# First table's rows eight ahead of the second table's, searches and a gelu moved with them

## The reference

```
def peer_ffn(xn, wq, keys1, keys2, U, V):
    ...
        q = (xc @ wq).reshape(B, C, PEER_HEADS, PEER_DQ)
        ...
        sc, ci = lax.top_k(cand, K)
        e = jnp.take_along_axis(i1, ci // K, axis=-1) * PEER_NKEYS + jnp.take_along_axis(i2, ci % K, axis=-1)
        g = jax.nn.softmax(sc, axis=-1).astype(xc.dtype)
        a = jax.nn.gelu(jnp.einsum('bchkd,bcd->bchk', U[e], xc), approximate=False)
        return jnp.einsum('bchk,bchkd->bcd', g * a, V[e])
```

## Time and profile before

| what | value |
|---|---|
| median of 3 runs | 2156.09 us (2155.67 to 2157.33) |
| the profiled execution's own time | 2158.93 us |
| its span, first to last instruction | 2157.2 us |
| busy PE / DVE / POOL / ACT | 86% / 60% / 34% / 27% of the span |
| gather queue q0 | 537.35 MB in 74176 packets, 60.1% of the 16 DMA engines' span |
| all DMA | 699.82 MB, mean 324 GB/s |
| granted TensorE clock, mean | 0.996 of full speed |

### The profile page before, as it was taken

The page is one execution under the profiler, slowest core; times in us unless marked ns, Lnnn a source line. Parts: engine busy times, 40 slices in busy tenths (PEclk is TensorE's granted clock), DMA queues, the critical chain, the costliest instruction groups (busy, mean ns, idle before and its releaser), DMA issues.

```text
span 2157.2 us, 22090 instructions
## 1 busy us (share of the span) xinstructions
PE 1864.7 (86%) x6535; PEld 1096.5 (51%) x6535; DVE 1286.2 (60%) x2142; ACT 588.8 (27%) x1064; POOL 728.2 (34%) x636
## 2 busy tenths in 40 slices
PE   9999999999999999999977777777777777777777
PEld 7888887777788786544423222222222222222222
DVE  5544556787866556776356556556556556546444
ACT  5544445555544443111111111111111111111101
POOL 2000011110000002755455445445455545545542
PEclk9999999999999999999999999999999999999999
DMA  7556743434456578999999999999999999999997
GB/s 266 190 186 198 225 150 108 146 108 136 139 180 236 188 237 309 398 412 403 421 422 420 422 421 422 422 422 422 422 422 422 422 422 422 422 422 421 422 422 329
DMA packets 164609, 699.82 MB, mean 324 GB/s; under 512 B 15633, under 2 KB 25905, under 8 KB 98257
## 3 DMA queue, kind: packets, MB, share of 16 engines
q0 software_dynamic: 74176, 537.35, 60.1%
q1 hardware_dynamic: 90384, 161.89, 23.4%
q10 hardware_dynamic: 2, 0.01, 0.0%
HBM read 697.10 MB, written 2.10 MB: 324 GB/s over the span
## 4 chain that ended last, share of the span: by engine, by line
PE 50%; DMA 38%; issue 5%; DVE 5%; POOL 1%; ACT 0%; DVEq 0%; POOLq 0%; ACTq 0%
DMA v_ring<-in_peer_v_dram,idx_v 31%; PE banks L1253 10%; PE banks L788 9%; PE banks L790 9%; PE banks L789 9%; DMA big<-in_peer_u_dram,idx_u 7%; PE banks L1222 4%; PE banks L764 1%; PE banks L1143 1%; DVE big L2358 1%; POOL v_ring L643 1%; DVE mx L1990 1%; DVE ws L1832 1%; DVE att L1987 1%; PE banks L1190 1%
## 5 line engine op out<-in xcount | busy, mean ns | idle before, releaser
L1253 PE MATMUL banks<-v_ring,kxT 128*128 128x512 f32 x1920 | 885.4, 605 | 266.7 <-DMA v_ring<-in_peer_v_dram,idx_v 265.7
L2358 DVE SCALAR_TENSOR_TENSOR big<-big,xn 128x2048 f32<-128x2048 f32 x256 | 586.9, 2293 | 417.4 <-DMA big<-in_peer_u_dram,idx_u 409.0
L1253 PEld LDWEIGHTS banks<-v_ring,kxT 128*128 128x128 f32 x1920 | 348.3, 190 | 801.3 <-ACT kxT L1736 390.2
L634 POOL DMA_INDIRECT big<-in_peer_u_dram,idx_u x256 | 369.9, 1445 | 203.8 <-DVE big L2358 109.2
L1832 DVE TENSOR_TENSOR ws<-wraw,ws 128x1024 fp32r<-128x1024 f32 (+1 forms) x248 | 294.6, 1194 | 210.2 <-ACT ws L1373 208.2
L643 POOL DMA_INDIRECT v_ring<-in_peer_v_dram,idx_v x240 | 283.0, 1179 | 404.5 <-PE banks L1253 360.4
L1736 ACT ACTIVATE kxT<-ident,ga 128x128 f32<-128x128 f32 x240 | 95.3, 401 | 954.6 <-PE banks L1253 951.8
L1373 ACT ACTIVATE ws<-wraw 128x1024 fp32r<-128x1024 f32 (+1 forms) x248 | 254.6, 1033 | 220.2 <-PE banks L790 202.8
L788 PE MATMUL banks<-ws,xr 128*128 128x512 f32 x736 | 294.5, 400 | 3.1 <-DVE ws L1832 2.2
L790 PE MATMUL banks<-ws,xr 128*128 128x512 f32 x736 | 287.3, 390 | 0.0
L789 PE MATMUL banks<-ws,xr 128*128 128x512 f32 x736 | 287.2, 390 | 0.0
(11 more groups left out here) (325 smaller groups left out, 1485.3 us busy)
## 6 DMA issues: line engine op xcount, KB each, us to landing
wraw<-in_w_in_dram SPq DMA_DIRECT2D x152, 512.0 KB, 3.5
wraw<-in_w_out_dram SPq DMA_DIRECT2D x32, 512.0 KB, 4.0
wraw<-in_w_xkv_dram SPq DMA_DIRECT2D x16, 512.0 KB, 6.8
wraw<-in_w_branch_da_dram SPq DMA_DIRECT2D x16, 512.0 KB, 3.9
wraw<-in_w_branch_nsa_dram SPq DMA_DIRECT2D x16, 512.0 KB, 4.1
wq<-in_peer_wq_dram SPq DMA_DIRECT2D x10, 512.0 KB, 14.5
wraw<-in_w_xq_dram SPq DMA_DIRECT2D x8, 512.0 KB, 3.6
wb<-in_peer_wq_dram SPq DMA_DIRECT2D x8, 512.0 KB, 6.9
```

The lines of the kernel that those rows point to most:

```text
L634: nc.gpsimd.indirect_dma_start(u_ring[:, r, :], None, peer_u[0], bass.IndirectOffsetOnAxis(ap=idx_u[par][:, j:j + 1], axis=0)).then_inc(u_ ...
L1253: last = nc.tensor.matmul(V_BANKS[c][n], diag[:, r, :], v_ring[:, r, n * NW:(n + 1) * NW], start=(first and j == 0), stop=(final and j == ...
L2358: V.scalar_tensor_tensor(out=u_ring[:, r, :], in0=u_ring[:, r, :], scalar=1.0, in1=xn3[:, par, :], op0=ALU.mult, op1=ALU.mult, accum_out=d ...
```

## The change

`U_LEAD` goes from 4 to 8, and four places follow it:

- in the hand-over, twelve U gathers instead of eight are mixed into the sixteen V1 gathers (all j but those with j % 4 == 3, instead of every second), so that it ends with U3.7 and no longer with U3.3;
- in the last unit the four odd V15 gathers stand at j = 9, 11, 13, 15 and no longer at j = 12 to 15;
- DVE's search for the next unit stands behind the products of slots 6 and 8 instead of 3 and 5 (from unit 3 on), and the softmax weights behind that of slot 13 instead of 9;
- ACT's gelu of unit u+1 stands behind twelve diagonals of unit u instead of sixteen (from V2 on; at V1 it was so already).

```diff
-U_LEAD = 4
+U_LEAD = 8
...
                             pool.wait_ge(v_used, UNITS * 16 + (RING - 32))
                             keep_indices(UNITS - 1, 1)
-                        fetch_last(2 * (j + U_LEAD - PK) + 1)
+                        if j % 2 == 1:
+                            fetch_last(j + U_LEAD - PK)
                     fetch_v(u - 1, j, 1 - par)
...
             for j in range(PK):
-                if j % 2 == 0:
+                if j % 4 != 3:
                     if ahead == PK:
                         pool.wait_ge(idx_ready, 4)
                     fetch_u(2 + ahead // PK, ahead % PK, ahead // PK)
...
                     route_softmax(u + 2)
-                    diagonals(par, u, range(5, PK))
+                    diagonals(par, u, range(5, 12))
                     gelu(1 - par, u + 1)
+                    diagonals(par, u, range(12, PK))
             act.wait_ge(ga_ready, UNITS - 1)
-            diagonals(0, UNITS - 2, range(PK))
+            diagonals(0, UNITS - 2, range(12))
             gelu(1, UNITS - 1)
+            diagonals(0, UNITS - 2, range(12, PK))
...
                     dot(u, par, j)
-                    if route_next and j == 3:
+                    if route_next and j == (6 if weigh_last else 3):
...
-                    if route_next and j == 5:
+                    if route_next and j == (8 if weigh_last else 5):
                         route_pairs(u + 1, 1 - par)
...
-                    if route_next and j == (9 if weigh_last else 13):
+                    if route_next and j == 13:
```

## The result

In runs on one chip, taken in turn, the changed kernel took 2164.39 us (median of 8, 2162.83 to 2167.06) and the kernel before 2157.51 us (median of 8, 2155.67 to 2160.13). The ratio is 1.0030, with a 95% interval of 1.0021 to 1.0039: slower by 0.3%, 6.5 us (4.5 to 8.4). The forecast was 5.0 us more than before; the spans of the two profiled executions, 2157.2 and 2164.3, differ by 7.1 us. The forecast of 2161.1 was made against a median of 2156.09. Against this comparison's own 2157.51 it is 2162.5, some 2 us short. On the forecast's own base the measured ratio gives 2156.09 x 1.0030 = 2162.6, inside the stated 2155.3 to 2164.3.

A forecast was written before the change was run, and what follows sets the result against it. The gathers' rate, 422 GB/s, was taken to bound the kernel from 1000 to about 2141 us. Profiled 2158.93 + 5.0 for one hand-over gap = 2163.9; against the median of 2156.09, forecast 2161.1 us, range 2155.3 to 2164.3.

The forecast's parts named there:

- What bounds: From 1000 to about 2141 us only the gathers' rate, 422 GB/s, sets the time; order matters only where the queue gaps.
- The parts with no cost: Steady lead of eight, moved searches and last unit: no cost; the last unit 0 to 0.6 us, taken as 0.
- Where and when POOL waits: Hand-over, near 1062 us: POOL waits 10 us or more to issue U3.4, 0.45 us before the gather ahead has landed.
- The size: Cost of U3.4's late issue in the hand-over: 5.0 us, lower bound 3.6, upper 6.1, or 6.7 with the last unit.
- together 1005 KB, which at 422 GB/s is 2.4 us: What the windows around V0.11, issued at 977.57, 3.1 us before the landing ahead, lack in the trace before the change.
- A's upper bound: A: one gap in the hand-over, 3.6 to 6.7 us, 2159.7 to 2162.8, chance 0.62; the upper bound is 6.7.
- the forecast's third way: Hand-over gap from the fastest gather, 7.5 us issue to landing: less its own 2.49, 5.0; 5.0 - 0.45 = 4.6 us.
- B: At U3.4 the queue outlasts the chain or a late issue costs only 1.6 us: 0 to 2 us, chance 0.28.
- the forecast's use of the rule: With the skill's 2.0 us of fixed cost, U3.4's gap in the hand-over would be 2.0 - 0.45 = 1.6 us.
- C: Over the full stretch the rate rises from 422 to 424 GB/s: 5.3 us faster, 2150.8, chance 0.05.
- D: Slower at each of 12 changes of unit, ACT holding four diagonals behind the gelu: 12 us at 1 each, 2168, chance 0.05.

The follow-up runs named there:

- gelu-behind-eight: Changed kernel with the gelu of unit 2 behind eight diagonals of V1 instead of twelve, in the hand-over alone: 2159.13 us against 2158.75 before, ratio 1.0000.
- spread kernels: Changed kernel with the hand-over's twelve U gathers placed later, at j = 0, 2, 4, 6, 8 and every j from 9 to 15: 2157.98 us, ratio 0.9999.
- the run with 11 diagonals: Changed kernel with the gelu of unit 2 behind eleven diagonals instead of twelve in the hand-over: 2163.57 us, ratio 1.0029 to the kernel before.
- ten diagonals: Changed kernel with the gelu of unit 2 behind ten diagonals instead of twelve in the hand-over: 2157.79 us, ratio 0.9999 to the kernel before.
- the last kernel: Kernel before the change, with U2.2 to U2.7 spread in pairs in front of V0.10, V0.11 and V0.12: 2157.09 us against 2158.98, ratio 0.9999.

## Why the prediction was right, and where it was short

**What bounds.** Right. The rate held at 419 to 424 in windows of 20 us, from 1000 to 1060 and from 1080 to 2100, and what is lost from 1060 to 1088 (6.6 us by windows, 7.0 to 7.9 by landings) is there at the last row (7.1). The rule drawn from it, that an order costs nothing unless the queue runs dry, is what the gelu-behind-eight and the spread kernels show: the order of the change or nearly so, no gap, no time.

**The parts with no cost.** Right for all three. The lead and the gelu's move cost nothing at a change of unit (422 in the steady stretch), and the run with the gelu back behind sixteen shows that the second is what keeps the first free. The searches' place has no effect that shows. The last unit costs nothing that can be told from spread: what is late at V1.13 is late by the same at the last odd slot.

**Where and when POOL waits.** Right to 0.3 us: forecast near 1062 with 10 us or more in front, found 1062.33 with 12.03; forecast 0.45 us ahead of the landing before it, found 0.40.

**The size.** Here the forecast was short. The term that was mis-sized is "together 1005 KB, which at 422 GB/s is 2.4 us", taken as the price of an issue 3.1 us ahead, with 2.65 added for 5.0. The gap measured 6.6 us by its windows and 7.1 by the last row; the ratio gives 6.5, and A's upper bound was 6.7. The run with 11 diagonals shows which half was off. Its issue comes 3.5 us earlier than the changed kernel's and saves 3.9 us by landings (7.9 - 4.0) and 2.3 by windows (6.6 - 4.3), so "2.65 later costs 2.65 more" holds roughly. The start of the sum does not: an issue 3.9 us ahead costs 4.3 us by the windows of the hand-over, where one 3.1 us ahead, later by that measure, had been priced at 2.4.

The two cases differ in POOL's own row. It takes 1.28 us for V0.11 and 2.93 and 2.94 for U3.4 with eleven and twelve diagonals, where DVE runs its products. The prediction saw this and put 1.1 us for it into the upper bound alone, not into the sum. With the measured difference, 2.94 - 1.28 = 1.66, the sum would have been an estimated 5.0 + 1.66 = 6.7. This is read from the traces and not tested: no run has U3.4 late with DVE idle. The first part of the loss is near what the forecast's third way gave, "the queue is dry 5.0 us after the issue without it"; its 7.5 us row is V0.11 itself.

| U3.4 issued ahead of the last landing | POOL's row | next V gather late | ahead + late | V1.13 late | windows lack, first and second dip | span against before (single executions) |
|---|---|---|---|---|---|---|
| 8.9 us (ten diagonals) | 2.93 | 0.0 | | 0.9 | | -1.5 |
| 3.9 us (eleven) | 2.93 | 1.7 | 5.6 | 4.0 | 3.2 and 1.1 | +3.9 |
| 0.4 us (twelve, the change) | 2.94 | 4.6 | 5.0 | 7.9 | 5.6 and 1.0 | +7.1 |
| -8.7 us (sixteen, each unit) | 2.87 | 14.0 | 5.3 | | | +15.3 a unit, against the changed kernel |

The 0.9 us of the first row may be in the other two as well. Issue plus lateness is 5.0 to 5.6 us, whatever the distance: with a POOL row of 2.9 us, an issue has to start some 5.3 us before the landing ahead of it to keep the queue from running dry. By the windows the second dip is alike in both kernels. The second window of the earlier trace rows, with 313 GB/s at a DMA share of 0.91, may be its like in the trace of before: by 1 us from 982 it has 328, 246, 311, 369 and 401 GB/s, and the changed kernel from 1076 has 344, 270, 311, 369 and 369.

A count by landings in the trace of before seems to ask for a higher price, and misleads. U2.3's product starts at 980.68; that of U2.10, eleven gathers later and so due at 980.68 + 11 x 2.49 = 1008.1, starts at 1012.49, 4.4 us late and not 2.4. But between the two SyncE has another tensor loaded over the same DMA engines, 1.05 MB on its queue q1 by 1012 us, which takes 2.5 us at 422 GB/s:

```profile
1001.36 0.34 SPq L533 DMA_DIRECT2D gfin<-in_norm_final_g_dram  x1
```

Without it 1.9 us are left, and the 2.4 of the windows stands. The 4.4 us in the expectation of the last kernel has the same fault.

**The rivals.** *B*, no gap that matters, falls: the queue was exactly as deep as counted, and a late issue costs more, not less. The lead needed here is 5.0 to 5.6 us by the table, counted from the start of POOL's row. The Trainium skill, DMA: Bandwidth & Descriptors, section on the anatomy of one DMA on the GpSimd path, puts the fixed cost at about 2.0 us beside bytes / 436 GB/s, 4.4 us for 1 MB. Counted from the end of POOL's row the trace agrees: U3.4 in the changed kernel lands 1069.64 - 1065.27 = 4.37 us behind it, and with eleven and sixteen diagonals the same gather lands 4.72 (1066.97 - 1062.25) and 4.73 us (1170.75 - 1166.02) behind. The row of 7.5 us that the forecast held against the page is V0.11, issued while another gather was still moving. What the forecast's use of the rule left out is the row itself: an estimate by the page's 2.0 with it is 2.0 - 0.40 + 2.94 = 4.5 us for the wait, where 4.6 was found. What B named as its condition, issued 5 us ahead, is very near the border, and the kernel with ten diagonals lies beyond it. *C*: 422 in the window at 1500. Two windows of 20 us behind the gap do give 424, those at 1100 and 1200, where the kernel before has 421 and 420, but others give 419 and 420, and the slices from 1082 on stay within 2 GB/s of before; the rate did not rise. *D*: 421 to 423 in the slices from 1082 to the last but two, so no change of unit pays. Its mechanism is real all the same, as the run with sixteen shows; the four slots by which the gelu moved are what keeps it away.

What stays open is the second dip. It follows a dry queue in the changed kernel and with eleven diagonals, and the DMA engines are shown busy in it. The queue is not short of gathers: by 1076.5 POOL has issued U3.5, V1.12, U3.6 and V1.13, and the first of them lands at 1077.25. Issues back to back are not enough to bring it: the spread kernel issues seven gathers in a row from 1058.65 on and stays at 415 to 424. A queue that is dry for microseconds may not be needed: the last kernel shows 354 and 359 GB/s at shares of 0.98 and 0.99 with no window of 5 us from 975 to 1030 below 0.98, and one of 1 us, at 1002, at 0.66. Nothing was run that would tell its cause. What the length of POOL's row costs by itself is open too.

## What to carry to other kernels

When one queue is the bound, an order is judged by one number per gather: how long before the landing ahead of it can it be issued? Here 8.9 us cost nothing, 3.9 us cost about 4, and 0.4 us about 7, so a margin of half a microsecond in such a count is no margin, and moving ACT's gelu by two slots is worth the whole loss. Add to it what the issuing engine's own row takes, and look at what that row will run beside: the wait that makes an issue late can also bring the work that makes it slow. And count a gap both ways, by windows and by later landings, but look first at what else used the DMA engines in between: here 1 MB of another tensor made a gap of 2.4 us look like 4.4.

## What the runs showed of the hardware that was not expected

- The second dip, above: after a dry queue, 344 to 393 GB/s at a DMA share of 0.95 to 1.00, 1.0 to 1.1 us by the windows, and landings 1.4 to 3.3 us later still.
- The granted clock fell after PE had little to do: 0.50 in the window from 1070 to 1075, the 1.2 GHz level, with 5.87 us in which PE had been idle until 1072.30, and the pair V1.10 and V1.11 then took 9.01 us in place of 7.13. It cost no time that shows: PE is waiting for a gather again before 1081.58 and 1088.05.
- POOL's issue of one gather took 0.93 to 0.94 us in most rows where DVE ran no product, and 2.10 to 2.94 us in the rows from 1062.33 on, which began during a product; each of those ended 0.81 to 0.82 us behind the product's end. POOL's busy time fell by 29 us over the run with the same number of gathers, and the end shows none of it.
